# Wide 512-column matmuls for the output projections beside the second attention of a two-block decoder kernel

## What is computed

```
def second_block(x, rel_table, w_in, w_out, ...):
    h = rmsnorm_2(x, norm_attn[l])
    proj = h @ w_in[l]
    ...
    o_a = dilated_mixer(pA, tbl_a)
    o_b = moba_mixer(pB[:, :, 0] * Q_SCALE, pB[:, :, 1], pB[:, :, 2], tbl_b)
    o_c = nsa_mixer(q_c, kv_c, g_c, cmp_w1[l], cmp_w2[l], cmp_pe[l], tbl_c)
    x = x + jnp.concatenate([o_a, o_b, o_c], axis=-1) @ w_out[l]
    h = rmsnorm_2(x, norm_mlp[l])
    x = x + conv_ffn(h, w_up[l], conv_w[l], conv_b[l], w_down[l])
return rmsnorm_2(x, norm_final)
```

## Time and profile before

| | |
|---|---|
| median of 3 runs | 2746.74 us |
| profiled execution, its own time | 2746.81 us |
| its span | 2745.0 us |
| PE busy | 2709.1 us (99%) |
| DVE busy | 1948.7 us (71%) |
| ACT busy | 1332.9 us (49%) |
| POOL busy | 120.0 us (4%) |
| HBM traffic | 186 GB/s over the span |

### The profile page before, as it was taken

The page is one execution under the profiler, slowest core; times in us unless marked ns, Lnnn a source line. Parts: engine busy times, 40 slices in busy tenths (PEclk is TensorE's granted clock), DMA queues, the critical chain, the costliest instruction groups (busy, mean ns, idle before and its releaser), DMA issues.

```text
span 2745.0 us, 49048 instructions
## 1 busy us (share of the span) xinstructions
PE 2709.1 (99%) x16313; PEld 2384.3 (87%) x16313; DVE 1948.7 (71%) x3026; ACT 1332.9 (49%) x2133; POOL 120.0 (4%) x216
## 2 busy tenths in 40 slices
PE   8999999999999999999999999999999999999998
PEld 7888988888888888888888888798988888888887
DVE  8787877767757764456655675866798875688855
ACT  6755555544454443334444444644655443444453
POOL 0000000001010000000000020100000000000000
PEclk9999999999999999999999999999999999999999
DMA  6555544445564556655554454454555555555554
GB/s 214 178 175 177 191 153 150 152 172 182 182 214 149 188 184 224 210 205 214 213 188 187 180 209 170 146 174 143 175 184 186 195 178 189 197 187 185 188 179 167
DMA packets 83165, 503.24 MB, mean 183 GB/s; under 512 B 9674, under 2 KB 17914, under 8 KB 31504
## 3 DMA queue, kind: packets, MB, share of 16 engines
q1 hardware_dynamic: 79824, 490.77, 51.0%
q0 software_dynamic: 3120, 11.14, 1.3%
q10 hardware_dynamic: 144, 0.30, 0.0%
HBM read 500.02 MB, written 10.55 MB: 186 GB/s over the span
## 4 chain that ended last, share of the span: by engine, by line
PE 93%; DVE 4%; ACT 1%; issue 1%; DMA 1%; DVEq 0%; ACTq 0%; SPq 0%
PE PS L672 40%; PE PS L677 21%; PE PS L643 13%; PE PS L647 7%; PE PS L847 1%; PE PS L849 1%; PE PS L848 1%; PE PS L660 1%; PE PS L661 1%; PE PS L662 1%; PE PS L736 1%; DVE w L2016 1%; PE PS L1041 1%; ACT w L1312 0%; DMA w_raw<-in_w_C 0%
## 5 line engine op out<-in xcount | busy, mean ns | idle before, releaser
L2016 DVE TENSOR_TENSOR w<-w_raw,w 128x1024 fp32r<-128x1024 f32 (+2 forms) x916 | 1039.5, 1169 | 338.9 <-ACT w L1312 336.5
L1312 ACT ACTIVATE w<-w_raw 128x1024 fp32r<-128x1024 f32 (+2 forms) x916 | 886.8, 1007 | 348.6 <-PE PS L677 221.9
L672 PE MATMUL PS<-h,w 128*128 128x512 f32 x1648 | 393.8, 391 | 0.0
L672 PE MATMUL PS<-u,w 128*128 128x512 f32 x1492 | 359.5, 391 | 0.0
L672 PEld LDWEIGHTS PS<-h,w 128*128 128x128 f32 x1648 | 303.0, 188 | 59.3 <-issue 0.4
L643 PE MATMUL PS<-h,w 128*128 128x512 f32 x1328 | 342.8, 400 | 0.8 <-ACT w L1312 0.8
L672 PE MATMUL PS<-f,w 128*128 128x512 f32 x1392 | 332.2, 391 | 0.0
L672 PEld LDWEIGHTS PS<-u,w 128*128 128x128 f32 x1492 | 273.0, 188 | 52.1
L672 PEld LDWEIGHTS PS<-f,w 128*128 128x128 f32 x1392 | 255.9, 188 | 49.6
L643 PEld LDWEIGHTS PS<-h,w 128*128 128x128 f32 x1328 | 238.9, 188 | 58.9 <-issue 13.8
L677 PEld LDWEIGHTS PS<-h,w 128*128 128x128 f32 x1648 | 211.3, 191 | 8.0
(11 more groups left out here) (414 smaller groups left out, 3199.9 us busy)
## 6 DMA issues: line engine op xcount, KB each, us to landing
w_raw<-in_w_FU SPq DMA_DIRECT2D x88, 1024.0 KB, 4.8
w_raw<-in_w_UP SPq DMA_DIRECT2D x64, 1024.0 KB, 4.8
w_raw<-in_w_DN SPq DMA_DIRECT2D x64, 1024.0 KB, 4.9
w_raw<-in_w_FD SPq DMA_DIRECT2D x64, 704.0 KB, 4.1
w_raw<-in_w_G SPq DMA_DIRECT2D x32, 1024.0 KB, 4.8
w_raw<-in_w_Q SPq DMA_DIRECT2D x18, 1024.0 KB, 4.9
w_raw<-in_w_X SPq DMA_DIRECT2D x16, 1024.0 KB, 4.9
w_raw<-in_w_Y SPq DMA_DIRECT2D x16, 1024.0 KB, 4.9
```

The lines of the kernel that those rows point to most:

```text
L672: pe.matmul(PS[:, bank, :], w_hi[:, 2 * s + hf, k * P:(k + 1) * P], rhs[:, k0 + offs[hf] + k].rearrange("p a b -> p (a b)"), start=start a ...
L1312: act.activation(w_hi[:, 2 * s + hf, 0:n * P], w_raw[:, s, off * P:(off + n) * P], ACT.Copy)\
L2016: tt(w_lo[:, slot, 0:n * P], w_raw[:, s, off * P:(off + n) * P], w_hi[:, slot, 0:n * P].bitcast(F32), ALU.subtract).then_inc(lo_ready, 1)
```

## The change

All units of OC and all of OA but the two of t = 0, e = 0 take the wide form. `join` adds the second half of the bank to x by a linked addition ahead of the old one, except for those two units. The number of links in a trip of the DVE's loop goes from 2 to 6.

```diff
@@ project_c
-  half_unit(U0["OC"] + c // 2, f // 2, f % 2, SUB_O, 6 if f == 3 else 0, oc2, 0, True, True, wide=False)
+  half_unit(U0["OC"] + c // 2, f // 2, f % 2, SUB_O, 6 if f == 3 else 0, oc2, 0, True, True)
@@ project_a
-  half_unit(U0["OA"] + 2 * t + e, e, s, SUB_O, 4 * s, h2, 0, True, True, wide=False)
+  half_unit(U0["OA"] + 2 * t + e, e, s, SUB_O, 4 * s, h2, 0, True, True)
@@ join
-  def join(name, c, bank):
+  def join(name, c, bank, wide=True):
       dve.wait_ge(half_done, 4 + 2 * U0[name] + c + 1)
+      if wide:
+          link(tt(x[:, c, :], PS[:, bank, S:2 * S], x[:, c, :], ALU.add))
       tt(x[:, c, :], PS[:, bank, 0:S], x[:, c, :], ALU.add).then_inc(acc_free, 1)
@@ tile_b of DVE
-  join("OA", 4 * t + 2 * e, 0)
+  join("OA", 4 * t + 2 * e, 0, wide=e > 0 or not isinstance(t, int) or t > 0)
...
-  join("OA", 4 * t + 2 * e + 1, 4)
+  join("OA", 4 * t + 2 * e + 1, 4, wide=e > 0 or not isinstance(t, int) or t > 0)
@@ the loop over t = 1, 2
-  link.begin(t - 1, 2)
+  link.begin(t - 1, 6)
```

## The result

The changed kernel takes 2750.16 us (median of 20 runs, 2749.92 to 2751.42), the kernel before 2746.75 us (20 runs, 2746.27 to 2747.61). The ratio is 1.0013, 95% interval 1.0007 to 1.0019: slower, but within 0.2%. The profiled execution took 2750.01 us, its span is 2748.2 us.

What follows compares the result with a forecast made beforehand. PE was taken to bound the kernel, DVE counting only where PE waits. The profiled 2746.81 us plus 3.6 in OC (additions 4.43, gain -0.84) minus 1.0 in OA gave 2749.4 us, range 2747.0 to 2751.9.

Steps and rivals of the forecast that it cites:

- What bounds the kernel: In OC and OA, PE savings count in full; DVE work costs only where PE waits for it.
- The addition, 0.46 us on the path: At 30 joins, one more DVE addition ends the join 0.46 us later, costing only where PE waits.
- Ten places: In OC, PE waits on DVE: nine additions in full and one for 0.29, 4.43 us.
- OA hides its additions: In an OA tile, DVE's work of 10.95 us fits into PE's 11.02, so additions cost nothing.
- The first rival: DVE becomes the bound of OA too: 14 joins add 6.4 us, giving 2755.8; chance 0.08.
- the tightest place: OA, head 1 of t = 1: scalings precede PE's need by 0.75 us, 0.23 left after the change.
- The gain of a unit, 0.07 us: Wide matmuls take 2.09 us a unit against 2.16; over 30 units 2.1 us at most.
- the sum, 2.6: Over both stages: OC +3.6 us and OA -1.0 us.
- The rule of the Trainium skill on the gap: Matmul gap N/2.4 + 2.5 ns: 16 ns saved a unit, 0.5 us in all; forecast went by the rows instead.
- Weight loads exposed: Rival: weight loads stand on PE's path, 180 fewer save 34.4 us, giving 2715; chance 0.02.
- additions hidden: Rival: additions nearly all hidden from PE, only the 2.1 us gain left, giving 2744.7; chance 0.08.
- What would show it: Profile signs: unit pitch 2.09 us, OC 56.5, OA 43.3 without PE waits, L2843 waits in OC 3 or 4.

Runs made afterwards that it cites:

- kernel 4: Against the kernel before: all units narrow, plus a linked addition into a buffer nobody reads at the same 30 joins; 2751.48 us, ratio 1.0016.
- Kernels 5 to 7: 5: changed kernel, unit 3 not waiting for unit 2's join, 2748.47 us; 6: also next scalings before last join, 2746.43; 7: also unit 1 narrow, 2744.91.
- kernels 1: Changed kernel with OA put back to the narrow form and one addition, OC left wide; 2750.72 us, ratio 1.0013 against the kernel before.
- kernel 3: Changed kernel with only the old addition, second half of each bank left out of x; 2745.70 us, ratio 0.9994 against the kernel before.
- kernel 8: Kernel before, all narrow, with unit 3 not waiting for unit 2's join and next scalings ahead of the last join; 2745.54 us, ratio 0.9996.

## Why the prediction was right, step by step

- **What bounds the kernel.** Right. PE bounds both stages, and DVE counts only where PE waits for it: kernel 4 puts 30 more additions on DVE; OC gets 4.38 us longer and OA 0.07.
- **The addition, 0.46 us on the path.** Right. The pairs stand 0.46 us apart in the new joins, and unit 2's wait went from 0.19 to 0.65.
- **Ten places.** Right in sum: the forecast had 4.43 us of additions in OC, kernel 4 measured 4.38. Kernels 5 to 7 took the places away in groups: the two of unit 3 were worth 1.37 us in OC, the scalings and unit 1 of k = 3 together 2.17 (both figures hold the waits that stood there before the change), and the four of unit 2 the 1.64 between 6 and 7. The prediction named 3 or 4 us of listed waits on L2843; they were 4.8 us, in seven places. One was misjudged in what takes its place: with the scalings moved, unit 1 of k = 2 turned from just covered into a wait of 0.36, and that of k = 3 kept 0.32.
- **OA hides its additions.** Right, and close: DVE is busy 10.73 of 11.12 us in a tile, 10.95 was laid out by hand. The first rival (0.08) did not come. Four additions more raised DVE's busy time by 1.14 us and not by 4 x 0.46 = 1.84, so the sum of 9.59 and 1.84 said too much. At the tightest place of the earlier trace rows the scalings now end 1950.33 (start 1949.78, 0.55 long) and the transposes start at 1950.56: 0.23 us of slack. That this is the very figure of the forecast is in part luck: against the start of the tile DVE is 0.37 us later and PE 0.15 earlier, where 0.32 and 0.20 were laid out.
- **Two places in OA that the forecast didn't have,** both in the first tile and small. The second part of head 0 waits for `o2_free`, which DVE counts up after the three low parts behind the last join of OC. With two additions in that join the low parts end at 1932.50 + 1.08 = 1933.58, where PE wants to start at 1933.66:

```profile
1932.50 1.08 DVE L2722 TENSOR_TENSOR h<-PS,h 128x256 fp32r<-128x256 f32 x3
1933.66 0.36 PE L660 MATMUL PS<-h,w 128*128 128x256 f32 x1
```

  These nine matmuls then take 1.14 to 1.16 us to the next start in every kernel that has two additions in OC's last join, and 1.08 or 1.09 in every other. This is the 0.07 to 0.09 us of OA in kernels 1 and 4; that the wait for `o2_free` is the cause is read from the program and this pattern. The other is head 1: its transposes come 0.09 us behind the end of the scalings before the change (1935.14 + 0.55, then 1935.78) and 0.06 after it. So the tightest place was this one, and not head 1 of t = 1 as the prediction has it, and a unit ahead of it can give back 0.03 us at most.
- **The gain of a unit, 0.07 us.** This is the term that was mis-sized; on the average of a stage it measured 0.034 in OC and 0.039 in OA (kernel 3). The forecast priced a unit as if it ran in a long stream. Where it does, it keeps nearly the forecast: in t = 1 the first unit of head 1, which runs right behind the second of head 0, takes 1950.56 - 1948.46 = 2.10 us from its start to the next, against 1947.11 - 1944.95 = 2.16 before. The second, behind transposes, takes 2.29 us against 2.32. The rows show both units and the V product that follows, after the change and then before:

```profile
1948.46 1.55 PE L643 MATMUL PS<-h,w 128*128 128x512 f32 x6
1949.84 0.88 PE L647 MATMUL PS<-h,w 128*128 128x256 f32 x6
1950.56 0.49 PE L1041 MATMUL PS<-const,sb 128*128 128x128 f32 x3
1950.80 1.64 PE L643 MATMUL PS<-h,w 128*128 128x512 f32 x6
1952.28 0.88 PE L647 MATMUL PS<-h,w 128*128 128x256 f32 x6
1953.09 0.65 PE L1175 MATMUL PS<-pt,v2s 128*64 128x256 f32 x4
```
```profile
1944.95 0.28 PE L660 MATMUL PS<-h,w 128*128 128x256 f32 x1
...
1947.11 0.49 PE L1041 MATMUL PS<-const,sb 128*128 128x128 f32 x3
1947.35 0.36 PE L660 MATMUL PS<-h,w 128*128 128x256 f32 x1
...
1949.67 0.65 PE L1175 MATMUL PS<-pt,v2s 128*64 128x256 f32 x4
```

Most of the 30 units stand behind other work. Behind scores or the V product the same tile shows 2.20 against 2.25 or 2.26. In all a tile with four wide units got 0.18 to 0.19 us shorter, 0.046 a unit, and 0.046 is also what kernel 3 gives in OC over the 12 units that the forecast counted (0.55 / 12): the averages of 0.034 and 0.039 are lower still because at some places PE stands on DVE anyway. So OC got back 0.55 us where 0.84 was laid down, and OA 0.52 in place of 0.98. These two make 0.75 of the 0.8 us by which the sum, 2.6, fell short of 3.4. What makes a unit behind other work gain less was not settled.
- **The rule of the Trainium skill on the gap.** The Trainium skill (TensorE: Matmul & The Clock Gate, Back-to-back issue gap) made the gain 0.016 us a unit, the forecast 0.07; what kernel 3 measured, 0.034 to 0.039, lies between. The pitch of 512 columns is 1.38 / 6 = 230 ns in the rows above, not 216, so the formula doesn't hold here either.
- **Weight loads exposed** (0.02) and **additions hidden** (0.08): neither. Kernel 3 has 180 loads fewer and gains 1.1 us in the two stages, not 34.
- **What would show it.** OC 56.5 and OA 43.3 were named; they are 56.94 and 43.57. A second and third listed wait of the transposes did not appear: those of k = 1 and 3 stand 0.28 us late in the timeline, but the view of waits lists only the one of k = 2.

## What to carry to other kernels

A form that saves PE time but leaves more to evacuate is paid for where the next matmul needs the same bank: in this kernel the second addition costs its whole pitch there, 0.46 us against 0.03 to 0.06 saved. Decide it unit by unit, by what stands between a unit and the next use of its bank. And look first at what the waits ask for: two edits of order (a wait that asked for the join of another bank, scalings placed behind a join) made OC 1.39 us shorter without any wide matmul (1.2 us by the medians, whose interval still contains no change).

## What the runs showed that I had not expected

- A unit's saving depends on what runs ahead of it: 0.06 us behind another unit, 0.05 behind scores or a V product, 0.03 behind transposes.
- DVE can be busy 96% of a tile (10.73 of 11.12 us) beside a PE that never waits, since each bank is needed only one unit later.
- The order alone shortened OC by 1.39 us where the waits of PE on DVE listed in OC went down by about 0.7 (from 1.1 + 0.6 to 1.0). The view of waits understates a stall: before the change unit 0 of k = 2 takes 2.92 us to the next start, 0.76 more than its 2.16, and 0.60 is listed; and unit 1 of k = 3 starts 0.96 us behind its transposes, 0.68 in kernel 8, and nothing is listed.
